# Cached key and value pages of the decode attention: grouped issue order on the load queue

## The reference

```python
def diff_attend(q, k, v, q_pos, k_pos, lam):
    s = jnp.einsum('bqhcd,bkhcd->bhcqk', q, k) / math.sqrt(DIFF_HEAD_DIM)
    s = jnp.where(k_pos[None, :] <= q_pos[:, None], s, -jnp.inf)
    p = jax.nn.softmax(s, axis=-1)
    attn = p[:, :, 0] - lam * p[:, :, 1]
    return jnp.einsum('bhqk,bkhe->bqhe', attn, v)

def diff_sample(q, k, v, lam, k_pool, v_pool, page_table):
    k_past = k_pool[page_table].reshape(B, -1, DIFF_HEADS, 2, DIFF_HEAD_DIM)
    v_past = v_pool[page_table].reshape(B, -1, DIFF_HEADS, DIFF_V_DIM)
    k_all = jnp.concatenate([k_past, k], axis=1)
    v_all = jnp.concatenate([v_past, v], axis=1)
    return diff_attend(q, k_all, v_all, past + jnp.arange(T), jnp.arange(past + T), lam)
```

## Time and profile before

| | us |
|---|---|
| median of 3 runs | 4746.07 |
| the profiled execution's own time | 4747.85 |
| its span, first to last instruction | 4745.9 |
| PE busy | 4075.4 (86%) |
| DVE busy | 2046.7 (43%) |
| ACT busy | 1740.5 (37%) |
| mean granted TensorE clock | 0.927 of full |

### The profile page before, as it was taken

The page is one execution under the profiler, slowest core; times in us unless marked ns, Lnnn a source line. Parts: engine busy times, 40 slices in busy tenths (PEclk is TensorE's granted clock), DMA queues, the critical chain, the costliest instruction groups (busy, mean ns, idle before and its releaser), DMA issues.

```text
span 4745.9 us, 113485 instructions
## 1 busy us (share of the span) xinstructions
PE 4075.4 (86%) x49138; PEld 3547.3 (75%) x49138; DVE 2046.7 (43%) x4539; ACT 1740.5 (37%) x3551; POOL 513.7 (11%) x273
## 2 busy tenths in 40 slices
PE   7999997888877888877989999978878688888778
PEld 7999997677765565556989999967777655655578
DVE  6111112666645555543231111136666455565445
ACT  2000001666655665541110000026666565665311
POOL 5223220000000000010032222200000000000201
PEclk9999998899998999987999999978999999999789
DMA  3112111111114454343221111111111153544242
GB/s 136 68 68 77 72 63 66 34 41 38 40 49 132 121 165 138 96 135 125 92 82 72 68 68 75 66 59 35 48 39 31 56 159 95 167 138 128 93 140 87
DMA packets 222341, 410.46 MB, mean 86 GB/s; under 512 B 32146, under 2 KB 132500, under 8 KB 207764
## 3 DMA queue, kind: packets, MB, share of 16 engines
q1 hardware_dynamic: 206868, 313.75, 21.1%
q10 hardware_dynamic: 14976, 89.46, 4.7%
HBM read 296.39 MB, written 106.76 MB: 85 GB/s over the span
## 4 chain that ended last, share of the span: by engine, by line
PE 71%; DVE 12%; ACT 9%; issue 4%; DMA 2%; SPq 2%; POOL 0%; DVEq 0%; ACTq 0%
PE psum L2041 10%; PE psum L2043 10%; PE psum L2044 10%; PE psum L1365 4%; PE psum L1393 4%; PE psum L714 3%; PE psum L1596 3%; PE psum L1597 3%; PE psum L1598 3%; PE psum L1381 2%; PE psum L1129 2%; ACT arena L1169 2%; PE psum L711 2%; PE psum L785 1%; DVE arena L519 1%
## 5 line engine op out<-in xcount | busy, mean ns | idle before, releaser
L2041 PE MATMUL psum<-x_hi,w_parts 128*128 128x416 f32 x2640 | 933.9, 354 | 48.4 <-POOL w_parts L1962 22.3
L2044 PE MATMUL psum<-x_hi,w_parts 128*128 128x416 f32 x2640 | 927.0, 351 | 0.0
L2043 PE MATMUL psum<-x_lo,w_parts 128*128 128x416 f32 x2624 | 921.4, 351 | 0.0
L1974 DVE TENSOR_TENSOR arena<-psum,arena 128x416 f32<-128x416 f32 x330 | 195.1, 593 | 1238.7 <-PE psum L2044 1234.6
L333 ACT ACTIVATE arena<-arena 128x256 f32<-128x256 f32 x16 | 8.2, 514 | 1477.4 <-DVE arena L457 1477.4
L2041 PEld LDWEIGHTS psum<-x_hi,w_parts 128*128 128x128 f32 x2640 | 497.3, 188 | 56.1 <-POOL w_parts L1962 24.0
L2044 PEld LDWEIGHTS psum<-x_hi,w_parts 128*128 128x128 f32 x2640 | 497.9, 189 | 6.6
L2043 PEld LDWEIGHTS psum<-x_lo,w_parts 128*128 128x128 f32 x2624 | 494.9, 189 | 4.9 <-issue 0.6
L1272 DVE TENSOR_SCALAR_CACHE_REDUCE arena<-psum 128x512 f32<-128x512 f32 (+3 forms) x640 | 357.8, 608 | 302.2 <-PE psum L1365 162.6
L1393 PE MATMUL psum<-arena 128*128 128x128 f32 x2176 | 310.9, 285 | 64.1 <-ACT arena L1178 46.8
L1365 PE MATMUL psum<-arena 64*128 64x512 f32 (+3 forms) x1280 | 328.2, 617 | 39.8 <-DVE arena L1272 21.8
(11 more groups left out here) (352 smaller groups left out, 6814.3 us busy)
## 6 DMA issues: line engine op xcount, KB each, us to landing
out_proj_t<-arena ACTq DMA_DIRECT2D x66, 1040.5 KB, 4.2
arena<-in_cache_k SPq DMA_DIRECT2D x256, 256.0 KB, 2.9
arena<-in_cache_v SPq DMA_DIRECT2D x256, 256.0 KB, 3.0
arena<-in_w_in SPq DMA_DIRECT2D x66, 512.0 KB, 3.5
arena<-out_proj_t SPq DMA_DIRECT2D x96, 257.0 KB, 3.4
arena<-out_proj_t SPq DMA_DIRECT2D x24, 1024.0 KB, 6.0
x_res<-in_x SPq DMA_DIRECT2D x10, 1664.0 KB, 17.2
m_raw<-mixed_t SPq DMA_DIRECT2D x10, 1664.0 KB, 7.7
```

The source lines that it names most:

```text
L1974: dve.tensor_tensor(ost[:, b % 2, 1 + g * TG:1 + (g + 1) * TG], bank[q % banks_of(l)][:, 0:TG], RSTD[:, cols(g)], ALU.mult).then_inc(p_ev, 1)
L2041: pe.matmul(bank[q % n][:, 0:TG], w_hi[:, b % 3, k, :], x_hi[:, k, cols(g)], start=(k == 0), stop=False)
L2043: pe.matmul(bank[q % n][:, 0:TG], w_hi[:, b % 3, k, :], xl, start=False, stop=False)
L2044: mm = pe.matmul(bank[q % n][:, 0:TG], w_lo[:, b % 3, k, :], x_hi[:, k, cols(g)], start=False, stop=(k == KT - 1))
```

## The change

The order of SP's loads within a sequence is another; what is loaded, into which slots and after which waits, stays. The other engines' streams are the same. In the new order sequence b has: key pages 4 to 7; value pages 0 to 7; in odd sequences both maps of the next head; key pages 8 to 15; the value map; key pages 0 to 3 of sequence b + 1; value pages 8 to 15.

```diff
-        def value_sync(sp, l, b, q):
-            n = b * 4 + q // 4
-            if n >= 2 and q % 4 == 0:
-                sp.wait_ge(pv_done, n - 1)
-            pg = sp.value_load(ptab[0:1, b * NP + q:b * NP + q + 1], min_val=0, max_val=N_PHYS - 1)
-            sp.dma_start(vpg[:, n % 2 * 4 + q % 4, :], ins["cache_v"][bass.ds(l * N_PHYS + pg, 1)].rearrange("n p c -> (n p) c")).then_inc(u_v[n % 2], 16)
+        def values_sync(sp, l, b, gs):
+            for g in gs:
+                n = b * 4 + g
+                if n >= 2:
+                    sp.wait_ge(pv_done, n - 1)
+                for p in range(4 * g, 4 * g + 4):
+                    pg = sp.value_load(ptab[0:1, b * NP + p:b * NP + p + 1], min_val=0, max_val=N_PHYS - 1)
+                    sp.dma_start(vpg[:, n % 2 * 4 + p % 4, :], ins["cache_v"][bass.ds(l * N_PHYS + pg, 1)].rearrange("n p c -> (n p) c")).then_inc(u_v[n % 2], 16)
...
-        def load_map(sp, l, h, i):
-            if h and i == 0:
+        def load_maps(sp, l, h):
+            if h:
                 sp.wait_ge(s_ok, first(NT * (h - 1)) + 1)
-            sp.dma_start(kq[h % 2][:, i, :], map_rows(l, h, (Q_ROW, K_ROW)[i])).then_inc(c_kq, 16)
+            for i, r in enumerate((Q_ROW, K_ROW)):
+                sp.dma_start(kq[h % 2][:, i, :], map_rows(l, h, r)).then_inc(c_kq, 16)
...
             for b in range(NSEQ):
                 h = b // 2
-                ahead = b % 2 and h + 1 < HEADS
-                for p in range(KS, NP):
-                    keys_sync(sp, l, b, (p,))
-                    if p < KS + 8:
-                        value_sync(sp, l, b, p - KS)
-                    if ahead and p in (12, 14):
-                        load_map(sp, l, h + 1, (p - 12) // 2)
-                if ahead:
+                keys_sync(sp, l, b, range(KS, 8))
+                values_sync(sp, l, b, (0, 1))
+                if b % 2 and h + 1 < HEADS:
+                    load_maps(sp, l, h + 1)
+                keys_sync(sp, l, b, range(8, NP))
+                if b % 2 and h + 1 < HEADS:
                     load_values(h + 1)
                 if b + 1 < NSEQ:
                     keys_sync(sp, l, b + 1, range(KS))
-                for q in range(8, NP):
-                    value_sync(sp, l, b, q)
+                values_sync(sp, l, b, (2, 3))
```

More of the change, by code:

```diff
@@ L1001, in attn_ahead @@
             pT.wait(sp, NU - 1, sT_BO)
-            for i in range(2):
-                load_map(sp, l, 0, i)
+            load_maps(sp, l, 0)
             sp.dma_start(dmask[:, :], ins["dmask"]).then_inc(c_cst, 16)
```

## The result

The changed kernel takes 4805.26 us (median of 4 runs, 4799.27 to 4815.77). The ratio to the kernel before is 1.0141, 95% interval 1.0120 to 1.0162: 57 to 77 us slower, 67 in the middle. Forecast was slower by 41 us, with a range that ended at 62 us over the median of before; 67 lies above that end, at about 4813. The bare median of 4805.26 would still lie inside the range, but the difference is read from the ratio, which takes both kernels' runs together. The direction and the place were right, the size was not.

The account below looks back on a forecast made before the run. PE was taken as the bound in attention. Terms 36.6 + 2.8 - 7.2 + 9.0 = 41 us on the profiled 4747.85 gave 4789, forecast as 4787 us (+0.9%) because the median lies 1.8 lower; range 4758 to 4808.

Parts of the forecast that it names:

- The bound: In the attention stage PE was taken as the bound, busy 557 of 653 us in layer 0.
- Which page, where, how often: Key page 8 was to be late in sequences 1, 3 and 5 of both layers, six times.
- SP's way to page 8: In sequence 1 SP issues key page 8 at 1542.7, behind eight value pages and two maps; before, at 1534.8.
- Landing: In sequence 1 the second map lands at 1549.1 and key page 8 0.7 us behind it, at about 1549.8.
- Lateness in sum: Key page 8 is 6.1 us late (bounds 5.6 and 7.1) in six odd sequences: 36.6 us.
- Sequences 0 and 7: Without maps, key page 8 is 1.0 us late in 7 and 0.4 in 0: 2.8 us in both layers.
- What is given back: Other waits of PE shrink behind each of the six stalls, by 1.2 us each: -7.2 us.
- The clock: Behind each of the six holes PE runs 4 us at the low clock, losing 1.5 us: 9 us in all.
- Short or swallowed: Rival, 12%: key page 8 does not queue behind the maps (4746 to 4760), or more is given back (4763).
- Paid twice: Rival, 12%: low clock lasts 10 us or more each time, or another large transfer meets the burst; 4805 to 4813.
- No effect: Rival, 3%: old and new load order come out alike for PE, needing SP pages well under 1.1 us; 4746.
- Faster: Rival, 3%: waits for a sequence's last value pages go, up to 12 us, if key page 8 lands before 1543.7; 4734.

Follow-up runs that it names:

- the last experiment: The kernel before, with the page numbers of value pages 8 to 15 read into registers before SP waits for the value products: 4720.53 us, ratio 0.9959.

## Where the prediction was right, and where it failed

- **The bound.** Right: PE sets the time, and the whole cost of the change is PE standing still or running slowly. Its idle time in the stages grew by 53.6 us, 49.7 of them the new row of waits, and its busy time by 8.1 us.
- **Which page, where, how often.** Right: key page 8 in sequences 1, 3, 5 of both layers, with the first wait in sequence 1, and small ones in 0 and 7. That both maps and value pages are needed for it is shown by the two runs that take one of them away.
- **SP's way to page 8.** 12.2 us after PE's first transpose of page 3 was forecast, 12.6 measured (12.3 to 12.9; 0.1 more on the base of the table). In sequence 1 0.25 us of it is key page 7, issued 1.66 us behind that transpose instead of 1.41; in layer 1 it is steps between value pages of up to 1.45 us.
- **Landing.** This is the step that failed. I took 5.4 us for the first map, "the median of 16", and added 2.6 for the second, which gave page 8 a landing of 7.1 us after its issue; 8.4 was measured, 8.3 to 8.7 in the means of the four profiles with the pair in front of it and value pages issued at SP's usual pace, and 9.5 where they went out faster. Of the 16 maps behind that median only four had travelled in pairs. The one pair of which I had the row took 9.0 us from its first issue to its second landing; the first of the changed kernel took 9.5. With the pair as it was measured page 8 lands 8.1 us after its issue. I had that as the upper bound and did not take it, though it was the row nearest to what the change does.
- **Lateness in sum.** Both together: 7.8 us instead of 6.1, six times, 47.1 instead of 36.6. Above the bound of 7.1 that I had set. The bounds of my sum ended at +67, where the result came to lie, but I had cut the stated range at +62.
- **Sequences 0 and 7.** 2.8 forecast, 2.9 measured, and 0.5 more on page 9. The share of sequence 0 in layer 0 did not come.
- **What is given back.** Also wrong. I had put 7.2 us; nothing came back in the stretch for which I had put it. PE's waits in the 33 us behind the first hole (1558.7 to 1592 us) are those of the earlier trace rows:

```profile
PE psum L1392 <- ACT arena L1177: 1.7, 2, 0.9
PE psum L1380 <- ACT arena L1177: 0.7, 1, 0.7
```

The way from page 8 to page 15 is longer, not shorter. These waits are for results that follow from PE's own work. Farther on it is not settled: from page 15 to the next sequence's page 3 the six take 196.5 and 192.0 us in the two profiles of the changed kernel and 200.9 and 198.7 before, but 192.1 and 192.4 in the two runs with hardly a hole, so that the hole need not be what shortened them.
- **The clock.** Right in size: 9.0 forecast; from page 8 to page 15 it takes 114.4 us in the six sequences instead of 103.8, 10.6 in all, 1.8 each. The low clock lasted 2.8 to 5.3 us beyond the holes, 23.7 us in all, which at the 0.35 us per us of the earlier trace rows gives 8.3; measured it is 0.45 us per us.
- **Sum.** 47.1 + 3.4 + 0 + 10.6 = 61 us, and the stages show 61.7. That it agrees so closely is partly luck: the stretches that the sum leaves out differ too, by 6.0 us less between page 15 and the next page 3 in all sequences and by as much more elsewhere. The forecast sum was 36.6 + 2.8 - 7.2 + 9.0 = 41. Of the 20 us between them the landing and SP's steps make 10.5, the give-back 7.2.
- **The rivals.** "Short or swallowed" fell: pages queue behind the maps' bytes (halves of maps, 2.75 us less). "Paid twice" named the right total for a wrong reason: the low clock lasted 3 to 5 us behind each hole, not 10. "No effect" fell, since a value page costs SP 1.1 us as before. "Faster" fell as its condition said, since page 8 of sequence 1 landed 7.9 us after PE could have used it; but its target was real, as the last experiment shows: those waits go when SP's reading of page numbers is moved ahead of the wait.

Open: why page 8 lands after 6.9 us in one sequence and after 9.3 in another. What is issued behind it is excluded, and ACT issues no DMA within 10 us ahead of its landing in any of the six.

## What to carry to other kernels

A load that is on time only by slack must be costed by everything that is moved in front of it on its queue, issue time and bytes added together, and from the row in which the same transfers travelled together, not from the median of single ones. Two moves that each cost little can be dear in one: slack is spent once. Where the engine that waits is the bound and its other waits hang on its own work, count nothing as given back close behind the wait, and add the low clock behind each hole.

## What the runs showed that I had not expected

- Reading the page number is about half of what a paged load costs the issuing queue: eight DMAs follow each other at 0.6 us when their numbers are in registers, at 1.1 us otherwise. Moving the reading ahead of a wait made the kernel 0.4% faster.
- SP's issue time is not fixed: a pair of map issues took 0.91 us behind value pages (1.35 once in twelve, 1.32 in sequence 1 where the value pages went out early) and 1.08 to 1.74 ahead of them, and page steps are 1.4 us now and then instead of 1.1. What lengthens them is not shown.
- The low clock begins inside a hole of 6.4 to 8.8 us and lasts 2.8 to 5.3 us beyond it, in all twelve such holes of the two profiles of the changed kernel (1.3 to 2.4 us lost each).
